# Loading the token rows by column half behind half a weight piece, and three smaller moves, in a two-layer mLSTM and expert trunk

## The chip, the cores and the metric

The kernel runs on one core of one Trainium2 chip. The metric is the device time of one execution in microseconds, and lower is better. A comparison uses the median of several runs of each kernel.

## The reference, cut to what matters

Two layers work on 256 tokens of 1024 columns. Each layer normalises the rows, multiplies them by one wide input projection, runs two kinds of attention, and adds the result of an output projection. A feed-forward part follows: dense in the first layer, the best two of eight experts in the second.

```python
def reference(x, ...):
    h = x
    for layer in range(DEPTH):                      # DEPTH = 2
        y = _rmsnorm(h, norm_mix_g[layer])
        h = h + _hybrid_mixer(y, w_in[layer], ...)  # w_in: 1024 x 3592
        y = _rmsnorm(h, norm_ffn_g[layer])
        if layer % 2 == 0:
            h = h + _swiglu(y, ffn_w_gate, ffn_w_up, ffn_w_down)
        else:
            h = h + _moe_swiglu(y, w_router, moe_w_gate, moe_w_up, moe_w_down)
    return _rmsnorm(h, norm_final_g)

def _moe_swiglu(h, w_router, w_gate, w_up, w_down):
    ...                                             # combine: the two best experts' weights
    for e in range(N_EXPERTS):                      # 8
        out = out + combine[..., e:e + 1] * _swiglu(h, w_gate[e], w_up[e], w_down[e])
```

## The kernel before, in words

All weights pass through the core once, in **pieces** of 1 MB (128 partitions by 2048 numbers). SyncE (SP) loads them in a fixed order into six buffers, `raw`. ScalarE (ACT) copies a piece to `whi`, rounded to the matmul's number format (`split`, line 664), VectorE (DVE) writes the rest, `raw - whi`, to `wlo` (`split`, line 1093), and TensorE (PE) multiplies three times: high by high, low by high, high by low (`passes`, line 1620). `whi` and `wlo` have three buffers each, so a split waits until PE has used the piece three places earlier. The order on each engine is written out by hand, and semaphores link them: `arrived`, `hi_ready`, `lo_ready`, `piece_used`. A load into `raw` waits until DVE is done with the piece six places earlier.

**The start.** SP issues the first 128 rows of x, the next 128 rows, two halves of weight piece 0 (512 KB each, lines 374 and 377), and then the whole pieces 1, 2, 3 and so on (line 350). PE has no input yet and runs 30 empty matmuls (`keep_busy(BEFORE_X, 6)`, line 1633). It transposes the first four column tiles of both row tiles (`transpose_h`, line 1655) and runs 44 more empty ones (`BEFORE_PIECE`). ACT copies the transposed tiles (`hT_copy`, line 709), DVE makes their low parts (`hT_rest`, line 1135), and only then both split the halves of piece 0. PE multiplies by the first half of piece 0, transposes the other four column tiles, and multiplies by the second half and by piece 1 (`first_columns_out`). GpSimd (POOL) meanwhile fills seven blocks of a DRAM tensor with zeros (line 541).

**The gates.** The weight pieces of layer 0's mixer are counted by `i` = 0 to 13. PE forms the gate sums after piece 1. On DVE the gate arithmetic (`gate_rows`, lines 1228 to 1244, with two activations on ACT between) stands at `i` = 2, behind the split of piece 5, and the copy-out of the key columns (`evacuate`, line 1197) stands behind it. PE waits for both: `gate_columns` (line 1768) after piece 4 waits for the gates, and `pair_scores` (line 1805) behind it for the key columns.

**The experts.** Seven jobs run in a loop and an eighth stands alone (`rest_of_job`). A job has 42 pieces, `i` = 0 to 41: seven blocks of gate, up and down pieces, six pieces to a block. PE turns the hidden rows (`hid_transpose`, line 2062) once in each block. DVE has two further instructions in a block: the product of gate and up (line 1487), ahead of the split at `i` = 7, 13, 19, 25, 31 and 37, and the low part of the hidden rows (line 1481), after the split at `i` = 5, 11, 17, 23, 29 and 35. The last job's `rest_of_job` also adds four fetched sets of rows to h (`add_picked`, line 1535), after the splits at `i` = 24, 27, 30 and 33. POOL fetches these rows with four indirect DMAs (line 639).

**The end.** Tokens that overflow an expert's 128 places would need up to three more jobs. ACT, DVE, PE and SP each load the count of jobs into a register (`value_load`) and run a loop of three rounds that does its work only while `j < jobs`. In the profiled execution there was none to do. Then ACT squares the rows of h (line 689) and takes the root (line 699), DVE takes the reciprocal (line 1108) and writes y (line 1112), and SP stores it.

Of the kernel before, what the change touches and what calls it, by code (L numbers as in the profile page):

```python
# [26 lines left out]
P = 128  # L27
TT = 2
# [34 lines left out]
EXTRA = 3  # L63
HEAD_BANK = (4, 5, 0, 1)
GATHER_BANK = (2, 3, 4, 6)
BEFORE_X, BEFORE_PIECE, BEFORE_CHOICE, BEFORE_SLOTS = 30, 44, 36, 8
JOBS = E + EXTRA


# [22 lines left out]
def trunk(nc, x, w_in, b_igate, b_fgate, conv_w, conv_b, g_mlstm, g_sb, w_out,  # L92
# [5 lines left out]
    with ExitStack() as ctx:  # L98
# [3 lines left out]
        def sem(name):  # L102
            return ctx.enter_context(nc.semaphore(name))
# [110 lines left out]
        lo_ready = sem("lo_ready")  # L214
        piece_used = sem("piece_used")
        x_in = [sem("x_in0"), sem("x_in1")]
        small_in = sem("small_in")
        zero_ready = sem("zero_ready")
        ident_ready = sem("ident_ready")
# [121 lines left out]
        def _(sp):  # L341
# [21 lines left out]
            def mixer(l):  # L363
                n = MIX_BASE[l]
                for b in range(BLOCKS):
                    for half in range(2):
                        if (l, b, half) != (0, 0, 0):
                            cols(n + 2 * b + half, w_in[l], half, FIRST_COLUMN[b])
                for i in range(4):
                    two_rows(n + 2 * BLOCKS + i, w_out[l], 256 * OUT_PIECES[i])  # L370

            for t in range(TT):
                sp.dma_start(h[:, t, :], x[0, t * P:(t + 1) * P, :]).then_inc(x_in[t], 16)
            sp.dma_start(raw[:, 0, 0:PIECE // 2].rearrange("p (k n) -> p k n", k=2),
                         w_in[0][0:2 * P, FIRST_COLUMN[0]:FIRST_COLUMN[0] + FB]
                         .rearrange("(k p) n -> p k n", p=P)).then_inc(first_half_in, 16)
            sp.dma_start(raw[:, 0, PIECE // 2:].rearrange("p (k n) -> p k n", k=2),
                         w_in[0][2 * P:4 * P, FIRST_COLUMN[0]:FIRST_COLUMN[0] + FB]
                         .rearrange("(k p) n -> p k n", p=P)).then_inc(arrived[0], 16)
            mixer(0)  # L380
            n = FFN_BASE
            wg, wu, wd = ffn_w_gate[0], ffn_w_up[0], ffn_w_down[0]
# [265 lines left out]
        def _(act):  # L648
# [18 lines left out]
            def split_upto(i):  # L667
                while done[0] <= i:
                    split(done[0])
                    done[0] += 1  # L670
# [5 lines left out]
            def square(u, m):  # L676

                c, t = m // TT, m % TT
                n = 3 * TT * u
                if u == 0:  # L680
                    act.wait_ge(x_in[t], 16)
                elif u < 4:
                    act.wait_ge(h_ready, 4 * (u - 1) + m + 1)
                elif m < 2 * TT - 1:
                    act.wait_ge(part_done[m], jobs)
                else:
                    act.wait_ge(job_done, jobs + 1)
                cs = slice(512 * c, 512 * c + 512)
                act.activation(y[:, t, cs], h[:, t, cs], ACT.Square, scale=D ** -0.5,
                               accum_out=ssq[:, 2 * t + c:2 * t + c + 1]).then_inc(ssq_ready, 1)  # L690
                if c == 0:
                    act.wait_ge(ssq_ready, n + 2 * t + 1)
                    act.activation(ssq_eps[:, t:t + 1], ssq[:, 2 * t:2 * t + 1], ACT.Identity,
                                   bias=eps[:]).then_inc(ssq_ready, 1)
# [40 lines left out]

            def mixer(l):
                n, q, s = MIX_BASE[l], 2 * l, MIX_SEAM[l]
                if l == 0:
                    act.wait_ge(gT_in, 16)
                    hT_copy(s, 0, xT_hi)  # L740
                    act.wait_ge(first_half_in, 16)
                    act.activation(whi[:, 0, 0:PIECE // 2], raw[:, 0, 0:PIECE // 2], ACT.Copy
                                   ).then_inc(first_hi, 1)
                    act.wait_ge(arrived[0], 16)
                    act.activation(whi[:, 0, PIECE // 2:], raw[:, 0, PIECE // 2:], ACT.Copy
                                   ).then_inc(hi_ready, 1)
                    done[0] = 1
                    square(s, 0)
                    square(s, 1)
                    split_upto(n + 1)  # L750
                    hT_copy(s, 1, xT_hi)
                    square(s, 2)
                    root(s, 0)
                    square(s, 3)
                    root(s, 1)
                    act.wait_ge(wif_in, 16)
                    act.activation(wif_hi[:], wif[:], ACT.Copy).then_inc(wif_hi_ready, 1)
                    act.wait_ge(consts, CONSTS)
                else:
                    seam(s)  # L760
# [287 lines left out]
                rest_of_job(then_next=True)  # L1048
            loop.reg = E - 1
            scatter_matrix()  # L1050
            rest_of_job(then_next=False)
            act.wait_ge(table_ready, 1)
            jobs = act.value_load(table_i[0:1, 3:4], min_val=E, max_val=JOBS)
            with act.Fori(E, JOBS) as j:
                with act.If(j < jobs):
                    loop.reg = j
                    tables("silu_and_others")
                    for i in range(NSPLIT):
                        split(n + i)
                    start_of_job()  # L1060
                    rest_of_job(then_next=False)
# [10 lines left out]
        def _(dve):  # L1072
# [83 lines left out]
            def mixer(l):  # L1156
# [2 lines left out]
                    dve.wait_ge(hid_ready, DENSE_FULL + 1)  # L1159
                dve.memset(qkp[:, :, 0:3], 0.0).then_inc(dve_step, 1)  # L1160
                steps[0] += 1
                if l == 0:
                    dve.wait_ge(gT_in, 16)
                    hT_rest(s, 0)
                    dve.wait_ge(first_hi, 1)
                    dve.tensor_tensor(wlo[:, 0, 0:PIECE // 2], raw[:, 0, 0:PIECE // 2],  # L1166
                                      whi[:, 0, 0:PIECE // 2].bitcast(F32), ALU.subtract
                                      ).then_inc(first_lo, 1)
                    dve.wait_ge(hi_ready, 1)
                    dve.tensor_tensor(wlo[:, 0, PIECE // 2:], raw[:, 0, PIECE // 2:],  # L1170
                                      whi[:, 0, PIECE // 2:].bitcast(F32), ALU.subtract
                                      ).then_inc(lo_ready, 1)
                    done[0] = 1
                    split_upto(n + 1)
                    hT_rest(s, 1)
                    dve.wait_ge(ident_ready, 1)
                    token_diagonal(s)
                    dve.wait_ge(wif_hi_ready, 1)
                    dve.tensor_tensor(wif_lo[:], wif[:], wif_hi[:].bitcast(F32), ALU.subtract
                                      ).then_inc(wif_ready, 1)  # L1180
                    dve.wait_ge(consts, CONSTS)
                    split_upto(n + 2)
                else:
                    seam(s, n, n)
# [353 lines left out]
            def rest_of_job(then_next, with_picks=False):  # L1538
                for i in range(4, JOB_PIECES + (4 if then_next else 0)):
# [10 lines left out]
                            hid_low(f - 1)  # L1550
                    if i == JOB_PIECES - 3 and then_next:
                        gathered(1)
                    if with_picks and i in (24, 27, 30, 33):
                        add_picked((i - 24) // 3)
                    if i == JOB_PIECES - 1 and not then_next:
                        for c in range(2):
                            dve.wait_ge(o_hi_ready, loop.at("half", c + 3 - 2 * E))
# [36 lines left out]
                loop.reg, loop.per = j, PER_JOB  # L1594
                rest_of_job(then_next=True)
            loop.reg = E - 1
            rest_of_job(then_next=False, with_picks=True)
            dve.wait_ge(table_ready, 1)
            jobs = dve.value_load(table_i[0:1, 3:4], min_val=E, max_val=JOBS)
            with dve.Fori(E, JOBS) as j:  # L1600
                with dve.If(j < jobs):
                    loop.reg = j
                    one_hot(0)
                    for i in range(NSPLIT):
                        split(n + i)
                    start_of_job()
                    rest_of_job(then_next=False)
# [5 lines left out]
        def _(pe):  # L1613
# [31 lines left out]
            def transpose_h(s, half, t):  # L1645

                if s == 0:
                    pe.wait_ge(x_in[t], 16)
                else:
                    pe.wait_ge(h_ready, 4 * (s - 1) + 2 * half + t + 1)  # L1650
                if half == 1 and s < ROUTE_SEAM:
                    pe.wait_ge(hT_ready, 8 * s + 4)
                for c in range(4):
                    c0 = 512 * half + c * P
                    ins = pe.transpose(turned(s, half, c)[:, t * P:(t + 1) * P], h[:, t, c0:c0 + P],  # L1655
                                       ident[:])
                ins.then_inc(hT_ps, 1)

            def first_columns_out(i, half, s):

                if i:
                    pe.wait_ge(lo_ready, i + 1)
                hi, lo = (v[:, i % NSPLIT, :].rearrange("p (k n) -> p k n", k=4) for v in (whi, wlo))
                for two in range(2):
                    if i == 0:
                        pe.wait_ge((first_lo, lo_ready)[two], 1)
                    for c in range(4):
                        acc = ps[:, c // 2, 256 * (c % 2):256 * (c % 2) + 256]
                        for k in (2 * two, 2 * two + 1):
# [515 lines left out]
```

## Time and profile before

| what | before |
|---|---|
| median of 3 runs | 1448.1 us (1447.89 to 1449.35) |
| the profiled execution | 1448.66 us |
| its span, first to last instruction | 1446.6 us |
| busy: PE, DVE, ACT, POOL | 99%, 79%, 69%, 11% |
| mean granted clock of PE | 0.997 of full |
| moved by DMA | 446 MB, 308 GB/s over the span |

The span is 2.06 us shorter than the profiled execution's own time. Idle time of an engine that is not the bottleneck costs nothing, and a busy engine need not be at its peak. A row of the timeline gives start and duration in us, engine, line and operation, and in brackets how long the engine was idle before it and what ended that.

### The profile page before, as it was taken

The numbers are of one execution on the slowest core, as the hardware profiler recorded it, in microseconds if no ns is written. First come the engines' busy times: TensorE is split into PE (matmuls) and PEld (weight loads), VectorE is DVE, ScalarE is ACT, GpSimd is POOL, SyncE is SP. The second block draws the span as 40 slices with busy tenths as digits, with TensorE's granted clock in tenths as the row PEclk, the third lists the DMA queues.
The fourth block names the chain that finished last, engine by engine and source line by source line (L and its number), as shares of the span: only waits on it lengthen the run. The fifth ranks groups of instructions, "written<-read, shape, count | busy, mean of one in ns | idle before, by whom it ended". The sixth has DMA issues, their size and how long they took to land.

```text
span 1446.6 us, 20250 instructions
## 1 busy us (share of the span) xinstructions
PE 1426.6 (99%) x7633; PEld 1220.1 (84%) x7633; DVE 1144.7 (79%) x832; ACT 999.6 (69%) x845; POOL 152.0 (11%) x198
## 2 busy tenths in 40 slices
PE   8999999999999999999999999999999999999997
PEld 8888999998988888888888888888888888888885
DVE  4667655555667888888988888888889888888897
ACT  5776534345776677777777777777777777777775
POOL 4100000000100499800000000000000000002000
PEclk9999999999999999999999999999999999999999
DMA  9833555554544599999999999999999999999993
GB/s 366 286 129 133 176 179 197 162 185 164 182 141 136 181 402 393 394 393 390 369 376 394 381 372 391 378 361 389 392 366 381 390 374 376 389 388 365 394 395 121
DMA packets 188146, 445.99 MB, mean 308 GB/s; under 512 B 7712, under 2 KB 9896, under 8 KB 188096
## 3 DMA queue, kind: packets, MB, share of 16 engines
q1 hardware_dynamic: 183232, 429.94, 81.4%
q0 software_dynamic: 3568, 11.62, 2.2%
q10 hardware_dynamic: 1296, 3.75, 0.6%
q8 instruction: 33, 0.54, 0.2%
q14 instruction: 17, 0.14, 0.0%
HBM read 434.79 MB, written 10.49 MB: 308 GB/s over the span
## 4 chain that ended last, share of the span: by engine, by line
PE 88%; DVE 4%; DMA 3%; issue 2%; ACT 2%; SPq 0%; DVEq 0%; ACTq 0%
PE ps L1620 82%; DMA raw<-in_w_in_dram 2%; PE ps L2062 2%; ACT whi L664 1%; DVE wlo L1093 1%; DMA raw<-in_moe_w_down_dram 1%; PE ps L1820 1%; PE ps L2027 0%; PE ps L1655 0%; SPq L350 0%; DVE qkc L1214 0%; PE ps L1805 0%; PE ps L2031 0%; PE ps L1998 0%; PE ps L1824 0%
## 5 line engine op out<-in xcount | busy, mean ns | idle before, releaser
L1093 DVE TENSOR_TENSOR wlo<-raw,whi 128x2048 fp32r<-128x2048 f32 x404 | 924.4, 2292 | 230.1 <-ACT whi L664 228.1
L664 ACT ACTIVATE whi<-raw 128x2048 fp32r<-128x2048 f32 x404 | 774.8, 1919 | 346.2 <-PE ps L1620 325.8
L1620 PE MATMUL ps<-whi,xT_hi 128*128 128x512 f32 x1056 | 418.1, 396 | 0.8 <-DVE wlo L1093 0.6
L1620 PE MATMUL ps<-wlo,xT_hi 128*128 128x512 f32 x1056 | 412.0, 390 | 0.0
L1620 PE MATMUL ps<-whi,xT_lo 128*128 128x512 f32 x1056 | 411.1, 389 | 0.0
L1620 PEld LDWEIGHTS ps<-wlo,xT_hi 128*128 128x128 f32 x1056 | 198.2, 188 | 42.5
L1620 PEld LDWEIGHTS ps<-whi,xT_hi 128*128 128x128 f32 x1056 | 198.4, 188 | 41.3 <-issue 2.0
L1620 PEld LDWEIGHTS ps<-whi,xT_lo 128*128 128x128 f32 x1056 | 198.6, 188 | 38.8
L1620 PE MATMUL ps<-whi,hid_hi 128*128 128x512 f32 (+1 forms) x536 | 210.7, 393 | 0.0
L1620 PE MATMUL ps<-wlo,hid_hi 128*128 128x512 f32 (+1 forms) x536 | 208.8, 390 | 0.0
L1620 PE MATMUL ps<-whi,hid_lo 128*128 128x512 f32 (+1 forms) x536 | 208.7, 389 | 0.0
L1620 PE MATMUL ps<-xT_hi,whi 128*128 128x256 f32 x608 | 173.4, 285 | 1.6 <-DVE wlo L1166 1.5
L1620 PE MATMUL ps<-xT_lo,whi 128*128 128x256 f32 x608 | 172.0, 283 | 0.0
L1620 PE MATMUL ps<-xT_hi,wlo 128*128 128x256 f32 x608 | 172.0, 283 | 0.0
L1620 PEld LDWEIGHTS ps<-whi,hid_hi 128*128 128x128 f32 (+1 forms) x536 | 100.7, 188 | 21.9 <-issue 1.8
L1620 PEld LDWEIGHTS ps<-xT_hi,whi 128*128 128x128 f32 x608 | 116.6, 192 | 2.8 <-DVE wlo L1166 1.7
L1620 PEld LDWEIGHTS ps<-wlo,hid_hi 128*128 128x128 f32 (+1 forms) x536 | 100.6, 188 | 21.1
L1620 PEld LDWEIGHTS ps<-whi,hid_lo 128*128 128x128 f32 (+1 forms) x536 | 100.7, 188 | 20.1
L1620 PEld LDWEIGHTS ps<-xT_lo,whi 128*128 128x128 f32 x608 | 116.6, 192 | 0.2
L1620 PEld LDWEIGHTS ps<-xT_hi,wlo 128*128 128x128 f32 x608 | 116.6, 192 | 0.0
L639 POOL DMA_INDIRECT qsT<-o_by_slot,slot_out x1 | 2.2, 2169 | 712.2 <-DMA o_by_slot<-vm 712.2
L674 ACT ACT_TABLE_LOAD x31 | 39.8, 1283 | 2.3 <-PEq L2168 1.7
(273 smaller groups left out, 894.9 us busy)
## 6 DMA issues: line engine op xcount, KB each, us to landing
raw<-in_moe_w_gate_dram SPq DMA_DIRECT2D x112, 1024.0 KB, 7.4
raw<-in_moe_w_up_dram SPq DMA_DIRECT2D x112, 1024.0 KB, 7.6
raw<-in_moe_w_down_dram SPq DMA_DIRECT2D x112, 1024.0 KB, 7.4
raw<-in_w_in_dram SPq DMA_DIRECT2D x27, 1024.0 KB, 8.7
raw<-in_ffn_w_gate_dram SPq DMA_DIRECT2D x10, 1024.0 KB, 5.1
raw<-in_ffn_w_up_dram SPq DMA_DIRECT2D x10, 1024.0 KB, 5.1
raw<-in_ffn_w_down_dram SPq DMA_DIRECT2D x10, 1024.0 KB, 5.0
raw<-in_w_out_dram SPq DMA_DIRECT2D x8, 1024.0 KB, 5.1
```

The lines of the kernel that those rows point to most:

```text
L639: pool.indirect_dma_start(picked[t][c], None, o_by_slot, bass.IndirectOffsetOnAxis(ap=slot_out[:, t, c:c + 1], axis=0)).then_inc(picked_in ...
L664: act.activation(whi[:, i % NSPLIT, :], raw[:, i % NRAW, :], ACT.Copy).then_inc(hi_ready, 1)
L674: act.preload_act_table_set(name)
L1093: dve.tensor_tensor(wlo[:, i % NSPLIT, :], raw[:, i % NRAW, :], whi[:, i % NSPLIT, :].bitcast(F32), ALU.subtract).then_inc(lo_ready, 1)
L1620: ins = pe.matmul(acc, lhs, rhs, start=start and m == 0, stop=stop and m == 2, skip_group_check=True)
L1820: pe.matmul(z[:, 0:256], tri_neg[:], softp[:, a, 0:256], start=False, stop=False, skip_group_check=True)
L2062: ins = pe.transpose(ps[:, 4 + f % 2, k * P:(k + 1) * P], prod[:, k * P:(k + 1) * P], ident[:])
```

## The change

SP's order becomes: first half of piece 0, columns 0 to 511 of all 256 rows of x, second half of piece 0, columns 512 to 1023 of x, and piece 1 in two halves; piece 2 and on as before. `x_in[0]` and `x_in[1]` now stand for the column halves. ACT and DVE split the first half of piece 0 ahead of their work on the transposed rows, and piece 1 in halves around `hT_copy(s, 1)` and `hT_rest(s, 1)`. PE waits for each half of piece 1 by itself. The empty matmuls become 44 before x and 10 after. In the last job, ACT and DVE load the count of jobs ahead of `rest_of_job` (PE and SP as before), and `add_picked` moves to `i` = 15, 21, 27 and 33.

```diff
-BEFORE_X, BEFORE_PIECE, BEFORE_CHOICE, BEFORE_SLOTS = 30, 44, 36, 8
+BEFORE_X, BEFORE_PIECE, BEFORE_CHOICE, BEFORE_SLOTS = 44, 10, 36, 8
 # SP
-            for t in range(TT):
-                sp.dma_start(h[:, t, :], x[0, t * P:(t + 1) * P, :]).then_inc(x_in[t], 16)
-            sp.dma_start(raw[:, 0, 0:PIECE // 2] ...).then_inc(first_half_in, 16)
-            sp.dma_start(raw[:, 0, PIECE // 2:] ...).then_inc(arrived[0], 16)
+            def first_quarter(i, q, landed):
+                r0 = 512 * i + 256 * q
+                sp.dma_start(raw[:, i, q * PIECE // 2:(q + 1) * PIECE // 2] ...,
+                             w_in[0][r0:r0 + 2 * P, FIRST_COLUMN[0]:FIRST_COLUMN[0] + FB]
+                             .rearrange("(k p) n -> p k n", p=P)).then_inc(landed, 16)
+            def first_rows_in(c):
+                cs = slice(512 * c, 512 * c + 512)
+                sp.dma_start(h[:, :, cs], x[0, :, cs].rearrange("(t p) d -> p t d", p=P)
+                             ).then_inc(x_in[c], 16)
+            first_quarter(0, 0, first_half_in)
+            first_rows_in(0)
+            first_quarter(0, 1, arrived[0])
+            first_rows_in(1)
+            first_quarter(1, 0, second_half_in)
+            first_quarter(1, 1, arrived[1])
 # ACT, first_split(i, q, landed, ready) = wait, copy half q of piece i to whi
                 if l == 0:
+                    first_split(0, 0, first_half_in, first_hi)
                     act.wait_ge(gT_in, 16)
                     hT_copy(s, 0, xT_hi)
-                    ... both halves of piece 0
+                    first_split(0, 1, arrived[0], hi_ready)
                     square(s, 0)
                     square(s, 1)
-                    split_upto(n + 1)
+                    first_split(1, 0, second_half_in, second_hi)
                     hT_copy(s, 1, xT_hi)
+                    first_split(1, 1, arrived[1], hi_ready)
 ...
             scatter_matrix()
-            rest_of_job(then_next=False)
             act.wait_ge(table_ready, 1)
             jobs = act.value_load(table_i[0:1, 3:4], min_val=E, max_val=JOBS)
+            rest_of_job(then_next=False)
 # DVE, first_split(i, q, split_high, n_high, ready) = wait, wlo = raw - whi for half q
                 if l == 0:
+                    first_split(0, 0, first_hi, 1, first_lo)
                     dve.wait_ge(gT_in, 16)
                     hT_rest(s, 0)
-                    ... both halves of piece 0
-                    split_upto(n + 1)
+                    first_split(0, 1, hi_ready, 1, lo_ready)
+                    first_split(1, 0, second_hi, 1, second_lo)
                     hT_rest(s, 1)
+                    first_split(1, 1, hi_ready, 2, lo_ready)
 ...
-                    if with_picks and i in (24, 27, 30, 33):
-                        add_picked((i - 24) // 3)
+                    if with_picks and i in (15, 21, 27, 33):
+                        add_picked((i - 15) // 6)
 ...
-            rest_of_job(then_next=False, with_picks=True)
             dve.wait_ge(table_ready, 1)
             jobs = dve.value_load(table_i[0:1, 3:4], min_val=E, max_val=JOBS)
+            rest_of_job(then_next=False, with_picks=True)
 # PE
-                    pe.wait_ge(x_in[t], 16)
+                    pe.wait_ge(x_in[half], 16)
 ...
-                if i:
+                if i > 1:
                     pe.wait_ge(lo_ready, i + 1)
 ...
+                    if i == 1:
+                        pe.wait_ge((second_lo, lo_ready)[two], 1 + two)
```

## Rows read from the trace of the kernel before

**Rows 1.** The page: busy us, share of the span and instructions of each engine.

```profile
PE 1426.6 (99%) x7633; PEld 1220.1 (84%) x7633; DVE 1144.7 (79%) x832; ACT 999.6 (69%) x845; POOL 152.0 (11%) x198
```

**Rows 2.** The chain that ended last, 0 to 47 us: start us, us, what.

```profile
7.95 26.23 DMA raw<-in_w_in_dram
...
38.47 0.43 DVE y L1228
...
45.06 1.22 DVE ksT L1197
```

**Rows 3.** The timeline of PE, 0 to 47 us.

```profile
6.19 0.66 PE L1655 MATMUL ps<-ident,h 128*128 128x128 f32 x4 [0.74 <-DMA h<-in_x_dram]
...
10.80 0.39 PE L1620 MATMUL ps<-xT_hi,whi 128*128 128x256 f32 x1 [1.50 <-DVE wlo L1166]
...
13.77 1.03 PE L1655 MATMUL ps<-ident,h 128*128 128x128 f32 x8
...
45.19 0.40 PE L1768 MATMUL ps<-ident,om 4*128 4x4 f32 x4 [0.74 <-DVE om L1244]
46.32 0.70 PE L1805 MATMUL ps<-qsT,ksT 64*128 64x256 f32 x4 [0.73 <-DVE ksT L1197]
```

**Rows 4.** The timelines of ACT and DVE, 6 to 11 us.

```profile
6.97 1.57 ACT L709 ACTIVATE xT_hi<-ps,gT 128x256 fp32r<-128x256 f32 x4 [3.97 <-PE ps L1655]
8.42 1.07 ACT L742 ACTIVATE whi<-raw 128x1024 fp32r<-128x1024 f32 x1
...
7.93 1.66 DVE L1135 SCALAR_TENSOR_TENSOR xT_lo<-ps,gT,xT_hi 128x256 fp32r<-128x256 f32 x4 [7.00 <-ACT xT_hi L709]
9.52 1.23 DVE L1166 TENSOR_TENSOR wlo<-raw,whi 128x1024 fp32r<-128x1024 f32 x1
```

**Rows 5.** The DMA issued at 2.18 us (KB, us to landing), and POOL's timeline.

```profile
raw<-in_w_in_dram SPq DMA_DIRECT2D x1, 512.0 KB, 6.7
...
13.78 3.70 POOL L541 DMA_DIRECT2D x_by_slot<-vs  x7
```

**Rows 6.** Windows: stretch, its us, busy per engine, granted PE clock, DMA share, GB/s.

```profile
44.30:46.30 2.00, 0.55 (x5) 0.32 (x4) 1.93 (x5) 2.00 (x2) 0.52 (x1) 1.00 1.04 383
...
473.10:475.00 1.90, 1.87 (x18) 1.88 (x19) 0.17 (x1) 1.90 (x5) 0.00 (x0) 1.00 0.45 94
475.00:478.50 3.50, 3.50 (x37) 3.36 (x36) 2.93 (x17) 2.44 (x2) 0.00 (x0) 0.54 0.67 253
```

**Rows 7.** The timeline of PE in the last job: where each block's transposes stand.

```profile
1364.93 0.60 PE L2062 MATMUL ps<-ident,scratch 128*128 128x128 f32 x4
...
1381.74 0.60 PE L2062 MATMUL ps<-ident,scratch 128*128 128x128 f32 x4
...
1399.11 0.60 PE L2062 MATMUL ps<-ident,scratch 128*128 128x128 f32 x4
...
1416.53 0.60 PE L2062 MATMUL ps<-ident,scratch 128*128 128x128 f32 x4
```

**Rows 8.** The timelines of DVE and POOL in the last job.

```profile
1389.34 1.28 DVE L1535 SCALAR_TENSOR_TENSOR h<-qsT,pick_w,h 128x1024 f32<-128x1024 f32 x1
...
1391.13 6.69 DVE L1093 TENSOR_TENSOR wlo<-raw,whi 128x2048 fp32r<-128x2048 f32 x3
...
1331.20 2.72 POOL L639 DMA_INDIRECT om<-o_by_slot,slot_out  x1 [0.30 <-issue]
```

**Rows 9.** The count load by its lines (ns: min/median/max), and both timelines behind it.

```profile
L1053 ACTq TENSOR_LOAD <-table_i x1: 477/477/477, 1434.8 to 1434.8; - x1
...
L1599 DVEq TENSOR_LOAD <-table_i x1: 548/548/548, 1437.4 to 1437.4; - x1
L1599 DVEq FUSED_REGOPS  x1: 220/220/220, 1438.0 to 1438.0; - x1
...
1440.08 0.29 ACT L699 ACTIVATE rms<-ssq,ssq_eps 128x1 f32<-128x1 f32 x1
...
1440.73 0.16 DVE L1108 RECIPROCAL rstd<-rms 128x1 f32<-128x1 f32 x1 [2.02 <-ACT rms L699]
```

More of the change, by code:

```diff
@@ L216, in trunk @@
         x_in = [sem("x_in0"), sem("x_in1")]
+        second_half_in = sem("second_half_in")
+        second_hi = sem("second_hi")
+        second_lo = sem("second_lo")
         small_in = sem("small_in")
@@ L366, in mixer @@
                     for half in range(2):
-                        if (l, b, half) != (0, 0, 0):
+                        if (l, b) != (0, 0):
                             cols(n + 2 * b + half, w_in[l], half, FIRST_COLUMN[b])
@@ L370, in mixer @@
                     two_rows(n + 2 * BLOCKS + i, w_out[l], 256 * OUT_PIECES[i])
-            for t in range(TT):
-                sp.dma_start(h[:, t, :], x[0, t * P:(t + 1) * P, :]).then_inc(x_in[t], 16)
[L374 to L379, printed above, removed]
+            def first_quarter(i, q, landed):
+                r0 = 512 * i + 256 * q
+                sp.dma_start(raw[:, i, q * PIECE // 2:(q + 1) * PIECE // 2].rearrange("p (k n) -> p k n", k=2),
+                             w_in[0][r0:r0 + 2 * P, FIRST_COLUMN[0]:FIRST_COLUMN[0] + FB]
[10 more added lines that the diff above has]
+            first_quarter(1, 1, arrived[1])
             mixer(0)
@@ L680, in square @@
                 if u == 0:
-                    act.wait_ge(x_in[t], 16)
+                    act.wait_ge(x_in[c], 16)
                 elif u < 4:
@@ L737, in mixer, with first_split @@
                 n, q, s = MIX_BASE[l], 2 * l, MIX_SEAM[l]
+                def first_split(i, q, landed, ready):
+                    v = slice(q * PIECE // 2, (q + 1) * PIECE // 2)
+                    act.wait_ge(landed, 16)
+                    act.activation(whi[:, i, v], raw[:, i, v], ACT.Copy).then_inc(ready, 1)
                 if l == 0:
+                    first_split(0, 0, first_half_in, first_hi)
                     act.wait_ge(gT_in, 16)
                     hT_copy(s, 0, xT_hi)
[L741 to L747, printed above, removed]
+                    first_split(0, 1, arrived[0], hi_ready)
                     square(s, 0)
                     square(s, 1)
-                    split_upto(n + 1)
+                    first_split(1, 0, second_half_in, second_hi)
                     hT_copy(s, 1, xT_hi)
+                    first_split(1, 1, arrived[1], hi_ready)
+                    done[0] = 2
                     square(s, 2)
@@ L1161, in mixer, with first_split @@
                 steps[0] += 1
+                def first_split(i, q, split_high, n_high, ready):
+                    v = slice(q * PIECE // 2, (q + 1) * PIECE // 2)
+                    dve.wait_ge(split_high, n_high)
+                    dve.tensor_tensor(wlo[:, i, v], raw[:, i, v], whi[:, i, v].bitcast(F32), ALU.subtract
+                                      ).then_inc(ready, 1)
                 if l == 0:
+                    first_split(0, 0, first_hi, 1, first_lo)
                     dve.wait_ge(gT_in, 16)
                     hT_rest(s, 0)
[L1165 to L1173, printed above, removed]
-                    split_upto(n + 1)
+                    first_split(0, 1, hi_ready, 1, lo_ready)
+                    first_split(1, 0, second_hi, 1, second_lo)
                     hT_rest(s, 1)
+                    first_split(1, 1, hi_ready, 2, lo_ready)
+                    done[0] = 2
                     dve.wait_ge(ident_ready, 1)
```

## Prediction, made before the changed kernel was run

> **What bounds the kernel now.** I read the page first: PE is busy 99% of the span and DVE 79% [rows 1]. That says that only a change which shortens PE's own idle time, or the start and the end where PE has no work, can move the total; it does not say which wait to look at. So I read next the chain that ended last around the two places that the diff touches, then each engine's timeline there. In the chain the reader should see that the first 46 us are not PE's at all: the chain is the load of piece 5, issued at 7.95 and landed 26.23 us later, at 34.18, then its two splits, the gate arithmetic from 38.47, and the key columns at 45.06 [rows 2]. PE, which began its real work at 10.80, catches up with this chain and waits for it twice, 0.74 and 0.73 us, before 46.32 [rows 3]. From there to about 92 us the chain is PE's. In the last job it is mostly PE with two interruptions by DVE, and at the end it runs through DVE's sequencer.
>
> **The start, part by part.** PE's first product waited for three things in line: x landed, transposes, ACT's copies and DVE's low parts, and only then the split of half a piece (1.07 us on ACT, 1.23 on DVE) [rows 3, 4]. The change puts that split ahead. The order of landing now: DMAs of 512 KB land one after the other; the second landed at about 6.1 (PE's transposes start at 6.19 on it) [rows 3] and the fourth at 2.18 + 6.7 = 8.9 [rows 5], so 1.4 us each. The half piece takes the first place (4.7) and its splits are done by 4.7 + 1.1 + 1.2 = 7.0. The first column half of x takes the second place, 6.1. Eight transposes take 1.03 us [rows 3]: 7.2. ACT's copies start then, and DVE 0.96 us behind them (7.93 less 6.97) [rows 4]: 8.3. One low tile is a quarter of 1.66 us: PE can begin at 8.8, against 10.80. That is 2.0 us earlier. What follows keeps up: the second half of piece 0 has landed at 7.5 and is split by about 11.2, PE wants it at 12.6; the halves of piece 1 are split by about 14.1 and 17.0, PE wants them at 15.5 and 18.3. The two empty-matmul counts sum to 54 instead of 74, all in time when PE has nothing else.
>
> **Where those 2.0 us go.** Not to the end. They only let PE reach piece 4's end 2.0 us sooner, and what is late next is still piece 5 and the gates behind it. The first wait grows from 0.74 to 2.7 us, and PE's scores stay at 46.32 unless piece 5 lands at another time. Its load stands in SP's queue behind the same bytes (1 MB of x, 5 MB of weights), and POOL's seven blocks of zeros, issued from 13.78 on, share the DMA engines with it [rows 5]. Neither changes. SP issues one DMA more ahead of it, but piece 5 was issued 26 us before it landed, so the issue time is covered; without that cover it would cost a few tenths.
>
> Does the extra DMA cost time on the DMA engines themselves? The 512 KB loads landed 1.4 us apart, which is 512 KB at 375 GB/s with nothing left over for a fixed cost, so I take 0. The Trainium skill, page "DMA: Bandwidth & Descriptors", section "Anatomy of one DMA — SWDGE (gpsimd) path", gives each DMA a fixed part of about 2.0 us beside its bytes. By the page the sum would be up to 2.0 us more, by the row nothing more. The row is of queued loads, as here.
>
> **The clock.** The longer stall has a price of its own. PE now has next to nothing to do from 46.32 - 0.73 - 0.4 - 2.7 = 42.5 to 46.32, 3.8 us with four small transposes in it; before it was 2.0 us, and the granted clock stayed at 1.00, that is 2.4 GHz [rows 6]. The nearest row of a longer poor stretch is at 471.5 to 475 us: transposes, a wait of 0.56 us and products with 8 columns. There the clock fell at once behind it and stood at a mean of 0.54 over 3.5 us, so about 3.2 us at 1.2 GHz [rows 6]. After our stall PE is again the chain, so a half-clock stretch costs half of the part of it that PE works in: 3.2 / 2 = 1.6 us if it begins when PE does, half of that if it begins within the stall. Bounds: 0 (the clock stays) and 1.6. I take 1.2, because the new stretch is emptier than the one in the row and begins to count before PE resumes.
>
> The Trainium skill, page "TensorE: Matmul & The Clock Gate", section "HAM oscillation — how this bites in real kernels", lays the fall to long idle gaps between bursts. Our row speaks for more: the clock fell there with no idle gap over 0.56 us. By the page's rule alone the sum would be without the 1.2 us, because the transposes divide the stall.
>
> **The rows added in the last job.** Blocks without an addition stand 16.81 us apart (1364.93 to 1381.74); the two blocks with two additions each took 17.37 and 17.42 [rows 7]. So the four cost 0.56 + 0.61 = 1.2 us. I put this on those at `i` = 24 and 30: the one at 1389.34 has the product right behind it and then three splits back to back from 1391.13 [rows 8], which is a DVE that is behind, and PE's chain waits there. One addition takes 1.2 us of DVE, the product 0.6; a split takes 2.2 of the 2.8 us that PE needs for a piece. One extra piece of work of 1.2 us at a time is caught up over the next splits, which are three buffers deep; 1.8 in a row is not. The new places, 15, 21, 27, 33, are all of the kind that 27 and 33 are: one to a block and no product behind. The earliest runs at about 1389.34 - 9 x 2.8 = 1364. The last fetch was issued at 1331.20 [rows 8], and even the longest landing shown, 26.23 us [rows 2], brings it in by 1357. So -1.2 us. Bounds: -1.2, and 0 if four blocks with one addition lose 0.3 each.
>
> **The count loaded ahead.** At the end the load takes ACT 0.48 us and DVE 0.55 + 0.22 = 0.77 us [rows 9], followed on each by the three empty rounds, which stay. Both lie on the end: DVE's reciprocal began at 1440.73, though the root was done at 1440.08 + 0.29 = 1440.37 [rows 9], so DVE's sequencer was the last. Without the loads DVE is free 0.77 earlier, at 1439.96, and the root is done at 1439.89: -0.8 us. Bounds: -0.5 (only ACT's part counts) and -0.9. The loads now stand at the start of the last job, behind a table that POOL finished long ago. What queues behind them is a split on either engine; DVE lags at most 0.8 us there, less than the 1.2 of an addition, and the 0.6 us a piece that DVE has to spare hides it. Without that cover it would cost up to 0.8.
>
> **The sum.** Start 0, clock +1.2, additions -1.2, count -0.8: -0.8 us. The profiled execution took 1448.66 us, its span and 2.06 us around it, so it would take 1447.9; the median lies 0.56 lower, and I forecast 1448.1 - 0.8 = **1447.3 us**.
>
> **The rivals.**
> - *The clock stays.* Everything as above without the +1.2: 1446.1 us. For it: the transposes at 45.19 divide the stall, and the clock stood through 2.0 us before. Against it: the fall at 475.
> - *The start comes through.* Piece 5 lands about 2 us earlier, or the stall proves to be something else, and the 2.0 us reach the end with no longer stall and no clock loss: 1448.1 - 2.0 - 2.0 = 1444.1 us. Against it: the bytes ahead of piece 5 are the same.
> - *The additions cost the same in the new places*, and the clock falls: 1448.1 + 1.2 - 0.8 = 1448.5 us. For it: two of the four places are old ones that I only argued to be harmless.
> - *Piece 5 lands later*, by the fixed cost of one more DMA in the queue, 2.0 us as the upper end: the chain of the first 46 us moves with it one for one. With the clock loss, 1448.1 - 0.8 + 2.0 = 1449.3 us, slower than before; it decides from a landing 0.8 us late. Against it: the even spacing of the 512 KB loads.
>
> That the change doesn't start PE earlier I give no case of its own, since it would end at the time of the first rival.
>
> **How the numbers follow.** A measurement of this kernel can tell about 0.2%, 2.9 us, from no change: 1445.2 to 1451.0. Chances: forecast 0.38, the clock stays 0.27, the start comes through 0.15, the additions cost the same 0.10, piece 5 late 0.06, anything else 0.04. The range takes in the first four, from 1444.0 to 1448.7. Faster by over 0.2%: the third case with 0.15 and a twentieth for the second ending lower, 0.20. Slower by over 0.2% needs a landing 3.7 us late or something unseen: 0.04. Within: 0.76. The forecast's own range is 1446.8 to 1447.9.
>
> **What would show it.** PE's first product at about 8.8. Piece 5's split on ACT still at 34.2 and PE's scores at 46.3, with an idle time of about 2.7 us before line 1768; a clock under 1.00 between 45 and 50. All blocks of the last job 16.8 us apart, except the last short one. DVE's reciprocal right behind ACT's root, and its count load at about 1328. The prediction fails if the split of piece 5 moves, if that idle time is not there, or if blocks with one addition are longer than 16.8.

## The result, and the profile after

| | before | after |
|---|---|---|
| median, 22 runs each on one chip | 1448.8 us (1447.3 to 1449.5) | 1450.3 us (1448.1 to 1453.9) |
| ratio, 95% interval | | 1.0013 [1.0007, 1.0019] |
| profiled execution, its span | 1448.7, 1446.6 us | 1449.5, 1447.7 us |

By the ratio the change costs 1.9 us, where 0.8 us less was forecast. That is inside the 0.2% that a measurement of this kernel can tell from no change, but the time lies outside the forecast's range, and the interval is on the slower side. The upper end moved most: four of the 22 runs took over 1452 us, none of before did.

The page of the changed kernel, its busy line, is that of before [rows 1]; nothing can be read from it:

```profile
PE 1426.7 (99%) x7613; PEld 1221.1 (84%) x7613; DVE 1145.6 (79%) x833; ACT 999.8 (69%) x846; POOL 154.2 (11%) x198
```

The start on ACT and DVE, against [rows 4]. The half piece's splits now come first, then the copies of x's transposes:

```profile
4.99 1.06 ACT L755 ACTIVATE whi<-raw 128x1024 fp32r<-128x1024 f32 x1 [1.96 <-DMA raw<-in_w_in_dram]
7.75 1.57 ACT L723 ACTIVATE xT_hi<-ps,gT 128x256 fp32r<-128x256 f32 x4 [1.71 <-PE ps L1672]
...
6.08 1.23 DVE L1181 TENSOR_TENSOR wlo<-raw,whi 128x1024 fp32r<-128x1024 f32 x1 [5.14 <-ACT whi L755]
8.71 1.66 DVE L1151 SCALAR_TENSOR_TENSOR xT_lo<-ps,gT,xT_hi 128x256 fp32r<-128x256 f32 x4 [1.41 <-ACT xT_hi L723]
```

The timeline of PE, against [rows 3]:

```profile
6.59 1.06 PE L1672 MATMUL ps<-ident,h 128*128 128x128 f32 x8 [0.70 <-DMA h<-in_x_dram]
...
9.34 0.36 PE L1637 MATMUL ps<-xT_hi,whi 128*128 128x256 f32 x1 [1.13 <-DVE xT_lo L1151]
...
45.78 0.41 PE L1787 MATMUL ps<-ident,om 4*128 4x4 f32 x4 [2.83 <-DVE om L1261]
46.91 1.22 PE L1824 MATMUL ps<-qsT,ksT 64*128 64x256 f32 x4 [0.73 <-DVE ksT L1214]
```

PE's first product is 1.46 us earlier (9.34 against 10.80), yet its score products stand 0.59 us later (46.91 against 46.32), and they take 1.22 us where they took 0.70. The wait at the gates grew from 0.74 to 2.83 us. The chain that ended last says why they are later: piece 5 landed at 34.77 instead of 34.18 [rows 2].

```profile
6.78 27.99 DMA raw<-in_w_in_dram
34.78 0.02 issue
34.80 1.92 ACT whi L678
...
45.65 1.22 DVE ksT L1214
46.87 0.04 issue
46.91 1.22 PE ps L1824 x4
```

Windows of the same stretch (us, busy per engine, granted PE clock, DMA share, GB/s), against [rows 6]:

```profile
44.90:46.69 1.79, 0.41 (x4) 0.32 (x4) 1.72 (x4) 1.79 (x2) 0.52 (x1) 1.00 1.05 386
46.69:50.10 3.41, 3.19 (x15) 2.60 (x16) 3.41 (x3) 1.84 (x3) 0.00 (x0) 0.50 0.68 246
50.10:52.00 1.90, 1.90 (x9) 1.56 (x9) 1.16 (x1) 1.88 (x2) 1.18 (x2) 1.00 0.79 197
```

The clock fell behind the stall to a mean of 0.50, the 1.2 GHz level, for 3.41 us, and PE worked in 3.19 of them. What it cost is read from the distance to the next layer-0 score block: its mask transposes began at 62.67 before and at 64.74 after. From the first score products that is 16.35 us before and 17.83 after, so 1.48 us for the clock. In the eleven profiles of the study whose clock stays at 1.00 there, the same distance is 16.34 to 16.47 us. With 0.59 from the landing the change stands 2.07 us behind when it leaves the start.

The end, timelines of PE and of ACT and DVE in the last job, against [rows 7] and [rows 9]:

```profile
1349.87 0.60 PE L2081 MATMUL ps<-ident,scratch 128*128 128x128 f32 x4
...
1366.65 0.60 PE L2081 MATMUL ps<-ident,scratch 128*128 128x128 f32 x4
1383.46 0.60 PE L2081 MATMUL ps<-ident,scratch 128*128 128x128 f32 x4
1400.24 0.60 PE L2081 MATMUL ps<-ident,scratch 128*128 128x128 f32 x4
...
1439.96 0.29 ACT L713 ACTIVATE rms<-ssq,ssq_eps 128x1 f32<-128x1 f32 x1
...
1440.37 0.16 DVE L1124 RECIPROCAL rstd<-rms 128x1 f32<-128x1 f32 x1 [1.10 <-ACT rms L713]
```

The blocks stand 16.78 to 16.81 us apart, where two took 17.37 and 17.42. The last transposes of the job's hidden rows, at 1425.88 before, are at 1426.41: the lag shrank from 1.72 us at 1349.87 to 0.53. From there to the reciprocal it took 14.85 us before and 13.96 after. So the reciprocal is 0.36 us earlier than before, in this pair.

Behind it that gain is lost again. From the reciprocal to the end of the span it took 5.90 us before and 7.37 after. SP's four stores of y lie in that stretch, and one of their issues is slow: before, the second, while the third had to wait for DVE's y anyway; after, the third, which holds up the fourth. Timeline of SP, the slow issue before and after:

```profile
1442.37 0.80 SPq L453 DMA_DIRECT2D out_dram<-y  x1
...
1442.87 1.50 SPq L467 DMA_DIRECT2D out_dram<-y  x1
```

This is not scatter. In the five profiles of the study that load the count where it was, the stretch takes 5.63 to 6.20 us; in the nine that load it ahead, 6.55 to 7.47, in kernels with the old start as with the new. In all fourteen the slow issue ends 0.2 to 0.4 us behind the end of a 16 KB load of instructions, which looks like what SP waits for. That load begins 15.7 us behind the last transposes before and 15.9 after, so it didn't move with the reciprocal. And with the count ahead the last landing of the stores comes 0.6 us behind the one before it, where otherwise it is under 0.05; why is not shown.

### The profile page after: what moved, and what is told of

The parts are those of the page before. It is cut to its first block, busy times and chain, and to the rows that moved or that the text cites. A ratio compares the mean times of both kernels' runs of the same rounds, so it can differ in the third digit from the quotient of the medians.

```text
span 1447.7 us, 20215 instructions
## 1 busy us (share of the span) xinstructions
PE 1426.7 (99%) x7613; PEld 1221.1 (84%) x7613; DVE 1145.6 (79%) x833; ACT 999.8 (69%) x846; POOL 154.2 (11%) x198
## 4 chain that ended last, share of the span: by engine, by line
PE 90%; DVE 3%; DMA 2%; issue 2%; ACT 2%; SPq 0%; DVEq 0%; ACTq 0%
PE ps L1637 85%; DMA raw<-in_w_in_dram 2%; PE ps L2081 2%; ACT whi L678 1%; DVE wlo L1109 1%; PE ps L1839 1%; PE ps L2046 0%; PE ps L1672 0%; PE ps L1824 0%; DVE qkc L1231 0%; PE ps L2050 0%; PE ps L1650 0%; PE ps L2017 0%; PE ps L1843 0%; PE ps L1841 0%
```

## The experiments

Each was timed against the kernel before on its own chip; ratios carry 95% intervals, which are about 0.9 thousandths to either side (1.3 us). Only the edit that differs is shown.

**The end alone.** The kernel before with both moves of its last job.

```diff
-                    if with_picks and i in (24, 27, 30, 33):
-                        add_picked((i - 24) // 3)
+                    if with_picks and i in (15, 21, 27, 33):
+                        add_picked((i - 15) // 6)
...
-            rest_of_job(then_next=False, with_picks=True)
             dve.wait_ge(table_ready, 1)
             jobs = dve.value_load(table_i[0:1, 3:4], min_val=E, max_val=JOBS)
+            rest_of_job(then_next=False, with_picks=True)
```

> Only the additions moved to 15, 21, 27 and 33 and the count loaded ahead; the start as before. Stall theory (the start makes PE wait longer before the gates, and the clock falls behind that wait): these two moves are worth 1.2 + 0.9 us, as in the profile of the change, so 2.0 us faster than before. Rival (the moves of the end cost something that the one profile hides): no faster than 1 us.

Measured: 1447.35 us against 1448.62, ratio 0.9992 [0.9983, 1.0001], so -1.2 us.

**The start alone.** The changed kernel with its last job as before (the diff above, reversed).

> Only the start is changed. Stall theory: 1.5 + 2.0 = 3.5 us slower than before at the median, with the granted clock at half behind 46 us, and a wide spread from run to run. Rival (the end costs): 1.5 us slower or less.

Measured: 1452.34 us, ratio 1.0022 [1.0013, 1.0031], so +3.2 us (+3.7 by the medians). The loss is in the start; the end takes 1.2 us of it back. Its windows around the stall show a longer half clock than the change's own profile:

```profile
44.00:46.50 2.50, 0.59 (x4) 0.50 (x4) 2.40 (x5) 2.50 (x2) 0.52 (x1) 0.68 1.06 388
46.50:49.90 3.40, 3.11 (x15) 2.52 (x16) 3.40 (x3) 1.83 (x3) 0.00 (x0) 0.50 0.71 256
49.90:53.30 3.40, 3.40 (x13) 2.71 (x12) 1.55 (x2) 3.35 (x4) 1.54 (x2) 0.73 0.89 295
```

A mean of 0.68 over 2.5 us is 1.6 us at half clock, 0.73 over 3.4 is 1.8: with the 3.4 between them 6.8 us. The clock fell here inside the stall, and PE was the chain through most of what followed. Scores to the next score block: 46.79 to 65.43, 18.64 us against 16.35, so 2.3 us lost.

**The start alone, a second profile.**

> One more profile of the change with its end as it was, whose median was 3.7 us above the kernel before while its first profile showed 2.8. If the rest is half clock that lasts longer in most executions, this profile shows a stretch behind 45 us of 6.8 us or more and a mean clock of 0.993 to 0.995, and the score products of the first layer at half speed. If it is later landing, piece 5's split is later than 34.8 and the clock is as in the first profile.

Measured: 1450.45 us, mean clock 0.996. Its half clock began at 47.1 and lasted 3.4 us; piece 5's split on ACT stood at 34.79, and scores to next scores took 17.95 us, 1.6 lost. The miss is useful: the same kernel loses 1.6 us in one execution and 2.3 in another, by when the clock falls. Eight of the eleven timed runs of the start alone took 1451.9 to 1453.1 us at a mean clock of 0.993 or 0.994, where its profiled ones had 0.995 and 0.996. A thousandth of mean clock is 2.9 us at half clock, or up to 1.45 us of time, so those runs have some 3 to 6 us more of it than the first profile. None of them is the profiled one, so where in the kernel it lies is not seen. They need no longer stretch behind the stall than the 6.8 us above: the profiles of the study also show half clock for 3.4 or 6.8 us in the routing stage, where 6.8 cost two of them 0.7 to 0.8 us of time, and for 4.7 to 7.4 us at the very end, where PE has no work. The longest of each make 21 us, a mean clock of 0.993.

**Empty matmuls in the stall.** The change, with 44 empty matmuls on PE ahead of layer 0's gate columns.

```diff
+                        if i == 4 and l == 0:
+                            keep_busy(44, 4)
```

> The changed kernel with 44 empty matmuls in the wait before the gate columns of layer 0, about 2.5 us of work in a wait of 2.9. Stall theory: the clock stays full and the time comes to 2.0 us below before, with a spread as narrow as before. Rival one (the clock falls in the first 10 us, where the change has 20 empty matmuls fewer behind the transposes): no better than the change, 1.5 us above before. Rival two (piece 5 lands later): the same, with piece 5 split after 34.8.

Measured: 1448.79 us, ratio 1.0000 [0.9991, 1.0009]: 1.9 us below the change by the ratios (about 1.6 to either side), but not below before. Its clock stayed at 1.00 through the start, and its scores, at 46.11, took 0.70 us:

```profile
45.60 0.41 PE L1787 MATMUL ps<-ident,om 4*128 4x4 f32 x4
46.11 0.70 PE L1824 MATMUL ps<-qsT,ksT 64*128 64x256 f32 x4
```

Among its eleven runs none had a mean clock under 0.995. So the clock's fall goes with PE's idleness at this place, and the step is shown. Part of what was expected and did not come is in the profile's last job, where PE waited 0.75 us for a split whose piece came late, and behind its reciprocal, where 7.22 us follow; I tested neither.

**PE starts late again.** The change, with 60 empty matmuls instead of 10 ahead of the first product.

```diff
-BEFORE_X, BEFORE_PIECE, BEFORE_CHOICE, BEFORE_SLOTS = 44, 10, 36, 8
+BEFORE_X, BEFORE_PIECE, BEFORE_CHOICE, BEFORE_SLOTS = 44, 60, 36, 8
```

> The changed kernel with 60 empty matmuls instead of 10 behind the first transposes, so that PE begins its first product at about 10.9 instead of 9.4, where it began before the change. Stall theory: the wait before the gate columns shrinks from 2.9 to about 1.4 us, the clock stays full, and the kernel gets faster by starting later: 1.3 us below before (what the end's moves measured by themselves) plus at most 0.6 for the later landing of piece 5, so between 1447.3 and 1448.0, against 1450.3 for the change. Rival (what was lost lies in the DMAs of the start alone): it stays at 1450.3 or gets slower by 1.5.

Measured: 1448.66 us, ratio 0.9996 [0.9987, 1.0005], 2.5 us under the change by the ratios. Throwing the 1.5 us of earlier start away makes the kernel faster: they only lengthened the stall, and here the clock stayed at 1.00. Timeline of PE:

```profile
45.33 0.41 PE L1787 MATMUL ps<-ident,om 4*128 4x4 f32 x4 [0.87 <-DVE om L1261]
46.45 0.70 PE L1824 MATMUL ps<-qsT,ksT 64*128 64x256 f32 x4 [0.72 <-DVE ksT L1214]
```

**Zeros behind piece 5.** The change, with POOL's seven blocks of zeros held until piece 5 has landed.

```diff
+            pool.wait_ge(arrived[5], 16)
```

> The changed kernel with POOL's seven stores of zeros held back until piece 5 has landed. Stall theory: piece 5 was late only because the stores share the DMA engines, so it lands at about 23, PE finds the gates done, the wait before them is gone and the clock stays full; the 1.5 us of earlier start reach the end, and the whole is 2.0 + 1.5 + 1.5 = 5.0 us below before, if the stores now don't hold up the value rows at about 52. Rival (the gates are held by something other than piece 5's landing): the wait stays, and the time is that of the change.

Measured: 1446.25 us, ratio 0.9982 [0.9973, 0.9991]. That is -2.6 us by the ratio, half of what was expected, and 4.5 under the change. Piece 5 landed at 26.14, 8.6 us earlier than in the change's profile. Its split came only 2.9 us earlier, since it now waited for PE and no more for the DMA.

```profile
31.89 1.92 ACT L679 ACTIVATE whi<-raw 128x2048 fp32r<-128x2048 f32 x1 [6.53 <-PE ps L1638]
```

**The same on the kernel before.**

> The kernel before with the seven blocks of zeros held until piece 5 has landed. If they delay piece 5 by a share of the DMA engines, piece 5's split comes up to 1.5 us earlier than 34.2, PE's waits before 46.32 shrink by the same, and the total is 1.0 to 1.5 us less. If the order of landing alone sets piece 5, nothing moves.

Measured: 1448.19 us against 1448.70, ratio 0.9998 [0.9990, 1.0007]. Nothing measurable. Here too piece 5 landed early, at 25.43, but its split stood at 33.73, only 0.5 us earlier than before, after 7.22 us of waiting for PE. With the old start PE frees the buffer no sooner than that; with the new one it does at 31.89. So the same edit is worth 4.5 us on the new start and 0.3 on the old.

**Gates ahead of the split.** The change, with layer 0's gate arithmetic put ahead of piece 5's split on ACT, and the same edit on DVE.

```diff
-                        if i < 13:
+                        if i < 13 and (i, l) != (2, 0):
                             split_upto(n + i + 3)
...
+                        if (i, l) == (2, 0):
+                            split_upto(n + i + 3)
```

> The changed kernel with layer 0's gate arithmetic ahead of the split of piece 5 on ACT and DVE. Stall theory: the gates no longer wait for piece 5's landing, PE finds them done at the end of piece 4 (about 42.9), the stall and the clock loss are gone and the 1.4 us of earlier start reach the end: 1.3 + 1.4 + the old 1.5 us of waiting, so about 4 us below before, 1444.5. Rival (something else holds PE at 46): the wait stays and the time is that of the change.

Measured: 1445.28 us against 1448.89, ratio 0.9973 [0.9963, 0.9984]. Timelines of ACT and PE:

```profile
34.32 1.28 ACT L688 ACT_TABLE_LOAD   x1
35.61 1.92 ACT L678 ACTIVATE whi<-raw 128x2048 fp32r<-128x2048 f32 x1
```

```profile
43.20 0.41 PE L1791 MATMUL ps<-ident,om 4*128 4x4 f32 x4
43.53 0.70 PE L1828 MATMUL ps<-qsT,ksT 64*128 64x256 f32 x4
```

Piece 5 is split at 35.61, later than in any other kernel here, and PE never waits: its scores stand 2.8 us earlier than before. The stall was not the piece's, it was the gate arithmetic's, which stood behind a split in two queues.

**Gates first, with the old start and the new end.**

> The start as before, the two moves of the end, and layer 0's gate arithmetic ahead of the split of piece 5. Against the same order with the changed start this prices the changed start with the gates out of its way. Stall theory: 1.4 us slower than that kernel, since PE starts 1.4 us later and nothing absorbs it, so about 1446.0. Rival (the changed start is worth nothing or costs by itself): the same time or faster.

Measured: 1447.01 us against 1448.89, ratio 0.9986 [0.9977, 0.9995]. The changed start takes another 1.7 us off (1445.28 against 1447.01; 0.9 to 2.6 by resampling the runs of both) once its gates are out of the way. In the two profiles PE's first product lies 1.1 us apart and its scores 1.1 (43.53 and 44.64).

**Both cures.** Gates first and zeros late on the change.

> The change with both cures at once: the seven blocks of zeros wait for piece 5's landing, and layer 0's gates go ahead of the split of piece 5 on ACT and DVE. Gates first alone was 3.6 us under the kernel before, zeros late alone 2.4. If both cure the same thing, PE's wait at the gates, nothing is left for the second to cure and it is again 3.6 under, about 1445.2. If the zeros' bytes were also in the way of pieces that PE waits for elsewhere, it is below 1444.5.

Measured: 1444.66 us against 1448.70, ratio 0.9974 [0.9965, 0.9982]. The same as gates first alone (0.9973), so both cure the one stall, as the first of the two expectations had it. It is not told apart from gates first.

**The parts of the end, each alone.** The additions moved; then the count loaded ahead.

> Only the additions moved, the rest as before. My sum: 1.2 us faster, all blocks 16.8 us apart. Rival (the gain of 1.3 us measured for both moves of the end is the count's alone): no gain.

Measured: 1446.98 us against 1448.89, ratio 0.9987 [0.9978, 0.9996], -1.9 us with an interval from -0.6 to -3.2.

> The kernel before with the job count alone read ahead of the last job. The prediction's term is -0.8 us (bounds -0.5 and -0.9), so a ratio of about 0.9994. In the profile DVE's reciprocal comes right behind ACT's root. If the scatter of the last stores swallows it, the medians are alike while the distance from the last matmul to the reciprocal is still 0.8 us shorter.

Measured: 1448.44 us against 1448.70, ratio 0.9998 [0.9989, 1.0006], -0.3 us with an interval from -1.6 to +0.9. By the total this experiment is inconclusive. By its profile the step is there: from the last transposes, at 1425.68, to the reciprocal it takes 13.95 us, 0.90 less than before, and DVE is right behind ACT. Behind the reciprocal it takes 6.64 us, 0.74 more than before, so that 0.2 us is left at the end of the span:

```profile
1439.22 0.29 ACT L699 ACTIVATE rms<-ssq,ssq_eps 128x1 f32<-128x1 f32 x1
...
1439.63 0.17 DVE L1108 RECIPROCAL rstd<-rms 128x1 f32<-128x1 f32 x1 [1.10 <-ACT rms L699]
```

## Why the prediction was wrong

**PE starts earlier: right, a little too large.** 2.0 us forecast, 1.46 seen. The half piece landed at 4.90 instead of 4.7, x's first column half let PE begin at 6.59 instead of 6.1, and all behind it moved with it. Over the profiles it is 6.59 to 6.89.

**The start does not come through: right.** PE waited 2.83 us where 2.7 was forecast, at the place named. That the two numbers are so near is luck: PE came 0.5 us less early than forecast, and the piece 0.6 us later. The start put back late proves it from the other side, and gates first shows what it takes for the start to be worth something.

**"Neither changes", said of what stands ahead of piece 5: a failed step, of 0.7 to 0.9 us.** In the four profiles with the old order and the zeros in their place piece 5's split on ACT began at 34.20, 33.31, 33.74 and 33.88, a mean of 33.8. With the new order, zeros in place and gates behind the split it began at 34.80, 34.67, 34.79, 33.99 and 34.34, a mean of 34.5. The third of the first four was held by PE, its piece had landed at 33.00; by the landings the means are 33.6 and 34.5. That is the rival "piece 5 lands later", at less than half of its price.

The extra DMA is not the cause, and 0 for it was right. The fourth load of 512 KB, now x's second column half, was issued at 2.33 and landed 6.8 us later, at 9.15 (8.84 before, [rows 5]):

```profile
h<-in_x_dram SPq DMA_DIRECT2D x1, 512.0 KB, 6.8
```

From there the two halves of piece 1 took 2.71 us to land, and the whole piece took 2.71 before. The delay stands ahead of them: the first two loads landed at 5.0 and 6.6 on the mean of the profiles with the new order, and at 4.6 and 6.0 with the old. What failed is that the same bytes in another order land at the same time. Whether it is the half piece in the first place or the x rows cut into column halves wasn't told apart. The Trainium skill, page "DMA: Bandwidth & Descriptors", section "Anatomy of one DMA — SWDGE (gpsimd) path", gives a fixed part of about 2.0 us for a DMA on GpSimd's path. These loads are on SP's queue, and no such part shows between them.

**The clock, "so about 3.2 us at 1.2 GHz", bounds 0 and 1.6: a term of the right kind and too small.** The mechanism was right: the clock falls behind this stall, and with PE kept busy it doesn't. The size was not. I let the fall last as long as the one in the row that I had, and made its cost the upper bound. The three profiles with this stall lost 1.5, 1.6 and 2.3 us; once the clock was down for 6.8 us. The start alone measured +3.2 us, with 1.3 to either side; less 0.7 to 0.9 for the landing, that leaves 2.3 to 2.5 for the clock, twice the 1.2 forecast. One row doesn't bound how long the clock stays down.

The Trainium skill, page "TensorE: Matmul & The Clock Gate", section "HAM oscillation — how this bites in real kernels", lays the fall to long idle gaps. Taken as in the prediction, with the transposes dividing the stall, it has no fall here. The trace has one, with no idle gap over 2.83 us, and the measurement decides.

**The additions: right.** -1.2 forecast; 1.19 seen between the blocks of the changed kernel (a lag of 1.72 that became 0.53), -1.9 [-3.2, -0.6] measured alone.

**The count, -0.8: the failed step of the end.** Up to the reciprocal it was right: 0.89 and 0.90 in two profiles. But the prediction took that for the end of the kernel and followed nothing behind it. There the nine profiles with the count ahead take 7.06 us on the mean and the five others 5.93, 1.1 us more. So at the end of the span the term is not -0.8 but about nothing, +0.2 by these means. The totals agree: -0.3 [-1.6, +0.9] alone, and -1.2 [-2.5, +0.1] for the end as a whole, which is what the additions give by themselves. The slow store issue and the late last landing make up the 1.1 us; what ties them to the place of the count load is open.

**The sum redone.** From the profiles: landing +0.7 to +0.9, clock +1.5 to +2.3, additions -1.2, count +0.2, so +1.2 to +2.2 us; by the ratio it is +1.9, interval +1.0 to +2.7. The forecast lay 2.7 us below the ratio's result: 0.7 to 0.9 of it is the landing, 0.3 to 1.1 the clock, and 1.0 the count. No profile caught a run at a mean clock of 0.993. Seven of the eleven timed runs of the start alone have it, and no run of a kernel without the stall does, so the stall has a part in it; how the half clock of those runs is spread over the kernel was not seen.

## What to carry to other kernels

Making an engine ready earlier ahead of a wait that something else ends isn't free: on TensorE the longer wait can take the clock down, and that lasts past the wait. Before shortening a start, look at what stands in the queues in front of the next late thing: here a dozen small gate instructions, put ahead of one split of a weight piece, took the scores from 46.91 to 43.53 us. Bound a cost that is seen once in the trace by more than that one size. And follow a time saved near the end up to the last landing: 0.9 us saved ahead of the reciprocal were gone behind it.

## What the hardware showed unexpectedly

The same start, with the same stall, got half clock from 46.7 us, from 47.1 and from 44.9, for 3.4, 3.4 and 6.8 us. The routing stage, whose half clock stands in [rows 6], had it for 3.4 us in ten of the fourteen profiles and for 6.8 us in four, with the same work there in all.

3.5 MB of zeros written by POOL's queue delayed a load in SP's queue that was issued 6 to 7 us ahead of them. It landed at 34.78 in the change's profile and at 26.14 with the zeros held back, and with the old start at 34.18 and 25.43. The order of issue doesn't protect a load that is still queued. Between 21 and 33 us POOL's queue moved nearly twice the bytes of SP's; its packets were of 4 KB, those of SP's of 2 KB.

A store issue that takes 0.35 us took 0.70 to 1.61 us in the nine profiles with the count ahead and 0.48 to 1.09 in the other five, each time ending 0.2 to 0.4 us behind a 16 KB load of instructions.
